# Hybrid decoder trunk on one core: a shorter start, two borders with other waits, output weights split during attention

## The reference

```python
for l in range(2):
    mod = silu(c) @ w_ada[l] + b_ada[l]              # 9 conditions: prompt, 8 samples
    sh1, sc1, g1, sh2, sc2, g2 = split(mod, 6)       # 1024 each
    h = rmsnorm(x, g_norm1[l]) * (1 + sc1) + sh1
    p = h @ w_in[l] + b_in[l]                        # 1024 -> 22 tiles of 128 columns, padded
    mix = [mlstm(p), pool_mix(p), fox_attention(p, cache, page_table)]
    x = x + g1 * (concat(mix) @ w_out[l])
    h2 = rmsnorm(x, g_norm2[l]) * (1 + sc2) + sh2
    x = x + g2 * (relu(h2 @ w_up[l]) ** 2 @ w_down[l])
y = rmsnorm(x, g_final)                              # and k, v, logf, states of both layers
```

## Time and profile before

| | |
|---|---|
| Median of 3 runs | 2941.03 us (2939.86 to 2941.24) |
| Profiled execution | 2944.28 us, of which the span of the trace is 2942.5 us |
| Start block | 0 to 69.6 us |
| Projection, attention, output and MLP of layer 0 | 69.6, 424.8, 645.3 to 1517 us |
| The same of layer 1 | 1521, 1858.1, 2081.9 to 2942.5 us |
| TensorE busy | 2773.4 us |

### The profile page before, as it was taken

How to read it: one execution, slowest core, us unless ns; L and a number is a source line. 1 busy time by engine, 2 the same in 40 slices (tenths; PEclk the granted TensorE clock), 3 DMA queues, 4 the chain that set the end, 5 groups by cost and what they waited for, 6 DMA issues and landing times. The chain is left out here.

```text
span 2942.5 us, 48195 instructions
## 1 busy us (share of the span) xinstructions
PE 2773.4 (94%) x20428; PEld 2557.8 (87%) x20428; DVE 1193.3 (41%) x2073; ACT 659.9 (22%) x1124; POOL 430.5 (15%) x424
## 2 busy tenths in 40 slices
PE   5899987879999999999999999788899999999998
PEld 2799984559999999999999999545799999999998
DVE  2635523445632432423456354233664233242344
ACT  2425313432211111010133442333231010100111
POOL 0100103451000000000101000234400000000010
PEclk9999988989999999999999999798999999999999
DMA  7430037752122222111124101676302111111111
GB/s 278 146 110 30 30 139 266 274 181 74 55 86 86 80 83 75 58 44 51 58 106 118 51 30 63 240 272 232 117 30 87 57 44 51 43 51 51 43 58 67
DMA packets 98761, 295.36 MB, mean 100 GB/s; under 512 B 19414, under 2 KB 24407, under 8 KB 96099
## 3 DMA queue, kind: packets, MB, share of 16 engines
q1 hardware_dynamic: 98386, 291.49, 29.5%
q0 software_dynamic: 160, 0.79, 0.1%
HBM read 269.61 MB, written 22.63 MB: 99 GB/s over the span
## 5 line engine op out<-in xcount | busy, mean ns | idle before, releaser
L438 PE MATMUL PS<-hH,whi 128*128 128x352 f32 x1632 | 534.8, 328 | 11.5 <-DVE wlo L431 8.5
L438 PE MATMUL PS<-hL,whi 128*128 128x352 f32 x1632 | 525.7, 322 | 0.0
L438 PE MATMUL PS<-hH,wlo 128*128 128x352 f32 x1632 | 525.2, 322 | 0.0
L438 PE MATMUL PS<-aH,whi 128*128 128x352 f32 x1344 | 439.6, 327 | 9.2 <-DVE aL L386 9.1
L438 PE MATMUL PS<-aL,whi 128*128 128x352 f32 x1344 | 432.7, 322 | 0.0
L438 PE MATMUL PS<-aH,wlo 128*128 128x352 f32 x1344 | 432.3, 322 | 0.0
L426 POOL CAST whi<-raw 128x1024 fp32r<-128x1024 f32 x162 | 170.7, 1055 | 1723.3 <-PE PS L438 1336.3
L438 PEld LDWEIGHTS PS<-hH,whi 128*128 128x128 f32 x1632 | 308.3, 189 | 19.5 <-DVE wlo L431 8.7
L438 PEld LDWEIGHTS PS<-hL,whi 128*128 128x128 f32 x1632 | 309.0, 189 | 0.0
L438 PEld LDWEIGHTS PS<-hH,wlo 128*128 128x128 f32 x1632 | 308.0, 189 | 0.0
L771 PE MATMUL PS<-aH,whi 128*128 128x352 f32 x912 | 304.2, 334 | 1.9 <-ACT F L967 1.9
(11 more groups left out here) (350 smaller groups left out, 3850.3 us busy)
## 6 DMA issues: line engine op xcount, KB each, us to landing
KVp<-kv SPq DMA_DIRECT2D x256, 384.0 KB, 4.4
raw<-w_ff SPq DMA_DIRECT2D x128, 512.0 KB, 3.6
raw<-w_in SPq DMA_DIRECT2D x42, 512.0 KB, 3.5
wad_single<-w_ada SPq DMA_DIRECT2D x40, 512.0 KB, 3.5
wad<-w_ada SPq DMA_DIRECT2D x32, 512.0 KB, 5.0
wada<-w_first SPq DMA_DIRECT2D x12, 1024.0 KB, 8.6
x_spill<-x SPq DMA_DIRECT2D x2, 4224.0 KB, 14.5
raw<-w_out SPq DMA_DIRECT2D x16, 512.0 KB, 4.1
```

The lines of the kernel that those rows point to most:

```text
L438: last = nc.tensor.matmul(PS[:, 3 * p + part, 0:CW], w[:, k, :], a[:, k, part * CW:(part + 1) * CW], start=k == 0 and w is wh and a is hig ...
```

## The change

It does four things.

1. **Start block.** It has 8 blocks of `w_first` instead of 12 (SC1 first, then SH1), in four buffers, each load held until an earlier one has landed. `x` comes in two halves between them. ACT squares tiles 0 to 3 after block 1, 4 and 5 after block 2, 6 and 7 after block 3. The sum of squares stands beside block 5, the root and its inverse behind it, the spread beside block 6, `scale_and_gain` beside block 5. The sums' offsets stand beside blocks 2 and 3. `past_sums` sums, `g_final` and the page table for scalar loads come after the last block. Weight panels 0 and 1 and `par` are loaded there and split there, the low parts on DVE between the biases of blocks 6 and 7.
2. **Projection.** In layer 0 it begins with `scale_rows`; the sample columns come after tile 0. The eight tiles of G1 are computed here, so layer 0 has 24 tiles in eight groups of three, the first eight of them read as halves of the 256 wide blocks (128 x 8 pieces of 512 bytes). The places of groups are given in thirds of panels, in both layers. G1 of layer 0 is counted by `extra` and `taken_before` later on.
3. **Border to attention.** The store of `o_v` counts on `row_store`; SP no longer waits for it. DVE and ACT wait for it before they first write `Fb`.
4. **Border to output.** POOL makes `whi` of both `w_out` panels at the end of attention, DVE makes `wlo` of panel 0 before its last copy. In the next block `split_low(1)` stands after `mix_low(0, 3)`.

The core of the diff (functions that only moved, and renamed indices, are left out):

```diff
-    wada = [tile(f"wada{s}", [P, KT, 256], W0 + 8192 * s) for s in range(3)]
+    wada = [tile(f"wada{s}", [P, KT, 256], aL0 + 8192 * s) for s in range(4)]
-    BLOCKS = 12
+    BLOCKS = 2 * KT // 2
+    i_w, first_load, first_high, first_low = stream("in", lambda n: w_in[n:n + 1])
+    TURN = [BLOCKS // 2 + i for i in range(BLOCKS // 2)] + list(range(BLOCKS // 2))
+    SUMMED_AT, SPREAD_AT = 5, 6
+    squared_after = {1: (0, 1, 2, 3), 2: (4, 5), 3: (6, 7)}
+    OFFSETS_AT = {2: 0, 3: 1}
 # start block, SP
-                if i >= 3:
-                    sp.wait_ge(a_done, i - 2)
+                if i >= 4:
+                    sp.wait_ge(a_done, i - 3)
+                    sp.wait_ge(a_loaded[(i - 2) % 4], 16 * ((i - 2) // 4 + 1))
...
             ada(1)
+            sp.dma_start(suf[:], suffix).then_inc(i_suf, 16)
+            sp.wait_ge(a_loaded[0], 16)
+            rows_in(0)
+            sp.wait_ge(a_loaded[1], 16)
             ada(2)
-            sp.dma_start(suf[:], suffix).then_inc(i_suf, 16)
-            sp.dma_start(gfin[:], g_final).then_inc(i_in, 16)
-            sp.dma_start(ptab[:], pages).then_inc(i_in, 16)
-            sp.dma_start(x[:], xT).then_inc(i_in, 16)
-            for i in range(3, 8):
-                ada(i)
+            sp.wait_ge(i_x, 16)
+            rows_in(1)
+            sp.wait_ge(a_loaded[2], 16)
+            ada(3)
+            sp.wait_ge(i_x, 32)
             sp.wait_ge(i_seg, 3)
...                                   # eight stores of zeros, as before
+            ada(4)
+            ada(5)
+            first_load(sp, 0)
+            ada(6)
+            first_load(sp, 1)
+            ada(7)
+            sp.dma_start(par[:], params[0]).then_inc(i_par, 16)
             for l in range(LAYERS):
-                sp.wait_ge(i_sum, l + 1)
...
-            for i in range(8, BLOCKS):
-                ada(i)
+                sums_out(l)
 # start block, PE
+                if i == SUMMED_AT:
+                    pe.wait_ge(i_norm["added"], KT - 2)
+                    pe.wait_ge(i_norm["squared"], KT)
+                    sum_squares(pe, i_norm, ss, sq_last[(KT - 1) % 2])
+                if i == SPREAD_AT:
+                    spread_roots(pe, i_norm)
 # start block, DVE
+                for j in squared_after.get(i + 1, ()):
+                    add_square(dve, i_norm, j, ss, sq_last)
+                if i == BLOCKS // 2 - 1:
+                    dve.wait_ge(a_moved, BLOCKS // 2)
+                    scale_and_gain(SC1, nxt[:, NEXT["g1"]]).then_inc(a_padded, 1)
+                if i == SUMMED_AT - 1:
+                    dve.wait_ge(i_norm["rooted"], 1)
+                    nc.vector.reciprocal(rr[:], rr[:]).then_inc(i_norm["inverted"], 1)
+                if i == BLOCKS - 2:
+                    for n in range(2):
+                        first_low(dve, n)
 # scale_rows
-            if k == 1:
+            if k == 0:
                 sample_columns()
 # projection
+            first_cond, groups = G1, [(at_, range(3 * i, 3 * i + 3)) for i, at_ in enumerate((1, 4, 6, 9, 11, 14, 16, 19))]
+            loads_at = {2: (0,), 5: (1,), 6: (2, 3), 7: (4, 5), 8: (6,), 9: (7,)}
+        fold_after = {at_ + 2: g for g, (at_, _) in enumerate(groups)}
+            w_first[KT + i // 2][:, :, P * (i % 2):P * (i % 2) + P] if i < KT else w_ada[i - KT]
...
-                sp.dma_start(o_v[...], F[:, VC:VC + 3, :]).then_inc(late_store, 16)
-                sp.wait_ge(late_store, 80)
+                sp.dma_start(o_v[...], F[:, VC:VC + 3, :]).then_inc(row_store, 16)
+                sp.wait_ge(late_store, 64)
 # attention: DVE and ACT before the first write of Fb, POOL at the end, DVE before picked_out
+                        if j == 0 and half == 0:
+                            dve.wait_ge(values_out, 64)
...
+                for n in range(2):
+                    pool.wait_ge(out_loaded[n], 16)
+                    is_full(pool, ("turned", NU - 1, n, chunks(NU - 1) - 1))
+                    nc.gpsimd.tensor_copy(whi[n][:], raw[n][:]).then_inc(out_high, 1)
...
+                        is_full(dve, ("mixed", max(u for at_, u in enumerate(piece_user) if at_ % 6 < 2)))
+                        dve.wait_ge(out_high, 1)
+                        nc.vector.tensor_tensor(wlo[0][:], raw[0][:], whi[0][:].bitcast(F32), ALU.subtract).then_inc(out_split, 1)
                         picked_out()
 # output and MLP
-                split_high(pool, 0)
-                split_high(pool, 1)
...
-                    if k < 2:
-                        split_low(dve, k)
+                    if k == 3:
+                        split_low(dve, 1)
```

More of the change, by code:

```diff
@@ L678, in load_ada @@
                         sp.wait_ge(ada_rows, i - 2)
-                    sp.dma_start(wad[i % 3][:], w_ada[bass.ds(l * CONDS + i, 1)].rearrange("a p k n -> (a p) k n")).then_inc(ada_loaded[i % 3], 16)
+                    sp.dma_start(wad[i % 3][:], condition(i)).then_inc(ada_loaded[i % 3], 16)
                 for n in range(2, NPAN):
@@ L683, in _ @@
                         sp.wait_ge(N["low"], KT)
-                    for i in ada_at.get(n + 1 if n == 2 else n - 1 if n >= 5 else 0, ()):
-                        load_ada(i)
+                    for g in loads_at.get(n, ()):
+                        for i in groups[g][1]:
+                            load_ada(i)
                     if n == 8:
@@ L888, in turn_values, with condition_rows @@
                     last.then_inc(cacheable, 1)
[L890 to L894 removed]
+                def condition_rows(g):
+                    if g:
+                        pe.wait_ge(ada_taken, g)
+                    for at_, i in enumerate(groups[g][1]):
                         pe.wait_ge(ada_loaded[i % 3], 16 * (i // 3 + 1))
@@ L897, in condition_rows, with fold_rows, conditions @@
                             q = k % 4
-                            last = nc.tensor.matmul(PS[32 * q:32 * q + 9, 6, at:at + P], cs[:, k, :], wad[i % 3][:, k, :],
+                            last = nc.tensor.matmul(PS[32 * q:32 * q + 9, 6, P * at_:P * at_ + P], cs[:, k, :], wad[i % 3][:, k, :],
                                                     start=k < 4, stop=k >= 4, skip_group_check=True)
                         last.then_inc(ada_rows, 1)
-                def fold_rows(n):
-                    pe.wait_ge(ada_taken, n - 2)
-                    for i in ada_at[n]:
-                        at = P * (i - ada_at[n][0])
-                        nc.tensor.matmul(PS[:, 7, 16 * i:16 * i + 9], mid_rows[:, at:at + P], c("fold"), start=True, stop=True).then_inc(ada_folded, 1)
+                def fold_rows(g):
+                    pe.wait_ge(ada_taken, g + 1)
+                    for at_, i in enumerate(groups[g][1]):
+                        nc.tensor.matmul(PS[:, 7, 16 * i:16 * i + 9], mid_rows[:, P * at_:P * at_ + P], c("fold"), start=True, stop=True)\
+                            .then_inc(ada_folded, 1)
+                def conditions(at_):
+                    if at_ in fold_after:
+                        fold_rows(fold_after[at_])
+                    if at_ in rows_after:
+                        condition_rows(rows_after[at_])
                 if begun:
@@ L1009, in numerator, with take_rows @@
                         .then_inc(S["moved"], 1)
-                def take_rows(n):
-                    act.wait_ge(ada_rows, ada_at[n][-1] + 1)
-                    if n > 3:
-                        act.wait_ge(ada_folded, ada_at[n][0])
-                    m = P * len(ada_at[n])
+                def take_rows(at_):
+                    if at_ not in rows_after:
+                        return
+                    these = groups[rows_after[at_]][1]
+                    act.wait_ge(ada_rows, these[-1] + 1)
+                    if these[0]:
+                        act.wait_ge(ada_folded, these[0])
+                    m = P * len(these)
                     nc.scalar.activation(mid_rows[:, 0:m], PS[:, 6, 0:m], ACT.Copy).then_inc(ada_taken, 1)
@@ L1023, in _ @@
                 else:
-                    root(act, N)
                     modulate(act, N, SC1, SH1)
@@ L1785, in forget @@
                         is_full(act, key)
+                        if j == 0 and half == 0:
+                            act.wait_ge(values_out, 64)
                         if j and half == 0:
@@ L2223, in _ @@
                         pass
-    first = len(sems)
     for l in range(LAYERS):
```

315 lines of the change are left out of this document (159 added, 156 removed).

## The result

| | before | changed |
|---|---|---|
| Median | 2940.45 us (4 runs, 2935.41 to 2941.24) | 2920.05 us (4 runs, 2919.02 to 2925.12) |
| Ratio | | 0.9937, 95% interval 0.9925 to 0.995 |
| Profiled execution, span | 2944.28, 2942.5 us | 2925.12, 2923.2 us |
| Same kernel in two later sets | 2936.38; 2940.61 | 2924.36 (0.9955, 0.9939 to 0.9971); 2925.49 (0.9957, 0.994 to 0.9974) |

The account below looks back on a forecast made before the run. TensorE, busy 2773 of 2942 us, was taken as the bound, so border savings should move the end: −15.3 − 11.7 + 5.6 − 2.9 − 5.2 = −29.5 us, from 2941.0 to 2911.5 us; 2903.5 to 2921 held eight in ten.

Parts of the forecast that it names:

- Start block, -15.3 predicted: Start block: reordered loads and shorter work let the next block begin at 54.3 instead of 69.6 us, bounds 51 to 60.
- Rival (a): Start block: loads leave gaps, each waiting for an earlier landing, so the block ends at 60; 2917 us, chance 0.10.
- Head of the projection, -11.7: Projection's beginning: 11.7 us removed from its head, 6.8 us stay, so the first panel matmul comes at 61.1.
- Eight tiles, +5.6: Projection of layer 0: eight more tiles on TensorE at 0.7 us each cost 5.6 us, bounds 5.0 to 6.8.
- Rival (g): Projection of layer 0: SP is held by the split tiles, 9.7 us each, making the kernel slower, 2958 us; chance 0.02.
- (d): Projection of layer 0: condition tiles come late from small pieces, 1 to 2.5 us per group of three; 2916 us, chance 0.08.
- (b): Borders to output: they give nothing, as DVE's chain of low parts replaces the split; 2916.7 us, chance 0.10.
- (c): Start block: loads run 15% below the 422 GB/s rate with fewer in flight, +4.4 us; 2915.9 us, chance 0.03.
- Border to attention, -2.9: Projection to attention, both layers: without SP's wait for `o_v` the next block begins 1.4 us earlier each; bounds 0 to 2.9.
- rival (e): Border to attention: the wait for `o_v` only moves to DVE, so nothing is gained; 2914.4 us, chance 0.05.
- Border to output, -5.2: Attention to output, both layers: splits made during attention let output matmuls start sooner, 2.6 us each; bounds 3 to 10.
- rival (f): Borders to output: TensorE's clock stays up at both, saving more than forecast; 2906.5 us, chance 0.12.

## Why the prediction was right and wrong

**Start block, -15.3 predicted, -7.4 found (-8.8 by the averages): the step that failed.** Up to half 1 of `x` the load model held: it lands at 27.2 (26.2 predicted). The next step, "then issues the zeros, 2.97 us", took its duration from a row in which the issues ended before their data moved: SP was through at 36.7, and the DMA share, 1.0 until 36, fell to 0.19 to 0.28 only from 38 to 46. The sums right behind them held SP 9.84 us. And "about 1 for the zeros on the same engines" took for granted that the bytes spread over 16 engines, where they lie in two rows of 16 KB. It cost 5.3 us of SP (8.25 for 2.97; 7.7 to 8.3 in the ten traces with the stores at this place). With it come 1 us of SP's earlier lateness and 1.5 us in the landing of block 4 (7.1 us after issue instead of 5.6), whose share between zeros and refilling is open. Block 4 lands at 42.7, not 34.8.

With sixteen rows the block ended at 53.1, which is before the forecast of 54.3. That is luck: block 4 landed at 36.3 there, 1.5 us late, and TensorE then ran faster than the prediction's rows of 1.94 and 2.77 us. At their pace, 19.2 us or more from block 4 to the next block, it would end near 55.6 (an estimate from the three slow traces). So the shape accounts for most of the miss and not for all. Rival (a) was near in size (60), and mostly wrong in cause: in the kernel with the zeros last each load still waits for an earlier one, and block 4 lands 5.3 us after its issue, with the DMA engines 91 to 111% busy by the record in every 2 us from 24 to 36. Only in two of the four kernels of that kind did it land later, by 1.8 and 2.1 us.

The Trainium skill has the rule that was missing, in DMA: Bandwidth & Descriptors, section Why a DMA increments its semaphore by 16 and not by 1: a DMA runs on the largest number of engines, up to 16, that divides the slowest dimension of both its sides. By it two rows go to two engines and sixteen to sixteen. The traces agree: two engines of 16 would be a share of 0.13, and it is 0.08 to 0.16 from 30 to 36 us; sixteen rows take 3.58 us for 8.25. That SP itself is held in issuing them is what the runs add.

The chain of the roots, the uncovered low parts (2.35 us of DVE) and the 0.5 us to the next block came as written in the profiled trace. The earlier place of the low parts removes 1.5 to 1.8 us, most of the saving of 2.1 that the prediction had seen (54.3 to 52.2) and the change had left.

**Head of the projection, -11.7:** right, 6.84 us remain for 6.8.

**Eight tiles, +5.6:** 6.7, inside 5.0 to 6.8 and near the upper end; the stretch is 284.5 to 285.7 us in twelve of the fourteen further traces of the new start and 282.8 in two (278.5 to 279.1 in the five of the old). No wait of TensorE for `wad` appears. Rival (g) had SP held 9.7 us a tile; the split tiles take it 0.67 us:

```profile
L726 SPq DMA_DIRECT2D wad<-w_first x8: 540/668/1289, 83.6 to 122.0; - x8
```

Rivals (d) and (g) are out. So is (b), by the border below. So is (c): up to half 1 of `x` the loads are 1.0 us late and not 15%.

**Border to attention, -2.9:** the step "`o_v` costs nothing, with 0.1 us to spare" held in part. The new wait shows in every trace with `o_v` in one store: the copy stands for `o_v` and not for TensorE. Yet with only the wait moved the copy came 1.5 and 2.5 us earlier, the predicted 1.4 or more, and in layer 1 of the changed kernel 2.0. In layer 0 of the changed kernel and its variants it was 1.4 to 1.5 earlier in five traces and 0.4 to 0.8 later than before in four, all three of the changed kernel itself among them. There the copy starts 7.2 to 7.6 us after the issue of `o_v`, which in the kernel before had landed 5.2 us after its own. That was rival (e), in these four. The prediction took the landing from a trace in which no load of attention ran beside `o_v`, and those loads now begin 1.6 us earlier. But they do so in the other seven traces too, so that they are the cause is not shown. In the time no gain can be told (0.9948 with the wait back in SP).

**Border to output, -5.2:** right, -5.5 in the profiled pair and 6.4 by the medians of all traces, and the clock hardly matters. In both layers of the profiled trace the half clock of the earlier trace rows is absent from the first output matmuls: TensorE takes a tile each 0.7 us, as DVE makes them, and stalls 1.38 us at tile 4. In 9 of the 20 stretches of the ten traces with this border and the low part on DVE the half clock is there. TensorE then takes a tile each 0.88 us, as predicted, and stalls 0.3 to 0.7 us (0.6 predicted). The stretches to the MLP's end come out alike, medians 869.4 and 869.8 us in layer 0, 848.0 and 847.9 in layer 1. So rival (f) was right that TensorE can stay at full clock there and wrong that it pays.

**Projection 1, 0 predicted, -1.25 found**, and -0.9 to -2.0 in all traces of the changed placing. But the two traces with the old placing and only `o_v` moved show 277.4 and 278.1 us as well, against 279.0 to 279.2 in the three of the kernel before: the placing is not shown to be the cause. The shorter ones have 3.4 us less at half clock there (6.8 for 10.2); what brings that is open.

**The rest is attention.** By the averages of all traces it is 6.8 us longer over both layers, where its border was to give 2.9: a miss of 9.7 us, larger than the start block's 6.5, if it is real. It would explain why the repetitions gave only 12.0 and 15.1 us. The prediction gave it one clause ("rises and falls on its own", 220.5 and 223.8); two values of one trace were too few to see that it moves by up to 10 us. The range of 2903.5 to 2921.0 held the first median, 2920.05, narrowly; the three ratios of the changed kernel, put on the scale of 2940.45, give 2921.9, 2927.2 and 2927.8 and lie outside.

## What to carry to other kernels

Before a small DMA is moved ahead of large ones, look at how many rows its slowest dimension has: to the queue that issues it, two rows of 16 KB were dearer here (8.25 us for eight such stores) than 128 rows of 8 KB (2.02 us for two such loads right behind them). The duration of an issue is that of the queue it was measured in, so a row can price it only if what is in flight around it stays the same. And price a stretch from several traces: traces of this start block differ by 3 us and those of attention by over 10, as much as most terms of the forecast or more. A transfer that has just been in time, as `o_v`, needs the same care: it was late in four of eleven traces.

## What the runs showed of the hardware

- Eight stores of 32 KB from two partitions held the issuing queue 7.7 to 8.3 us in two places of the list; from sixteen partitions 3.6 to 3.9 us. In the kernel before they took 2.97 us, and the eight stores of sums behind them 9.84; in the changed kernels those took 5.6 to 7.0. Together the two held it 12.8 us before, 13.2 to 14.9 with two rows, 9.9 to 10.7 with sixteen.
- Sixteen matmuls of 128x256 in the start block took 1.94 us in some traces and 1.07 in others, with a granted clock of 1.00 on record in both.
- Beside a POOL subtraction of 128x1024 (2.35 us) the first of DVE's low parts did not end before it did, where DVE makes one in 0.72 us on average (2.89 us for four in the changed kernel).
- Attention, with the same 2452 matmuls, took 271.2 to 285.9 us, with the granted clock at 0.92 to 0.87. An effect under 3 us there needs many traces.
